# Router of a mixture-of-experts trunk: one chain over all tokens, and one chain per block of 128 tokens

## What is computed

```python
def hier_moe(h, w_rg, w_re, w_gate, w_up, w_down):
    t = h.reshape(b * s, d)
    pg = softmax(t @ w_rg);  pg_top, g_idx = top_k(pg, 1)          # the best of 4 groups
    le = (t @ w_re).reshape(-1, 4, 8)
    le_sel = take_along_axis(le, g_idx[:, :, None], axis=1)[:, 0]    # its 8 experts
    pe_top, e_idx = top_k(softmax(le_sel), 2)                        # the best two of them
    w = pg_top * pe_top / sum(pe_top)
    ids = g_idx * 8 + e_idx
    combine = sum(one_hot(ids, 32) * w[..., None], 1)
    a = silu(t @ w_gate[e]) * (t @ w_up[e]) * combine                # for all experts e
    return sum over e of a @ w_down[e]
```

## Time and profile before

| | us |
|---|---|
| median of 3 runs | 1030.28 (1030.17 to 1032.45) |
| the profiled execution | 1029.97 |
| its span, first to last instruction | 1028.3 |
| TensorE busy | 961.8 (94%) |
| VectorE busy | 575.5 (56%) |
| ScalarE busy | 428.9 (42%) |
| DMA moved | 313.02 MB, 304 GB/s on the mean |

### The profile page before, as it was taken

The page is one execution under the profiler, slowest core; times in us unless marked ns, Lnnn a source line. Parts: engine busy times, 40 slices in busy tenths (PEclk is TensorE's granted clock), DMA queues, the critical chain, the costliest instruction groups (busy, mean ns, idle before and its releaser), DMA issues.

```text
span 1028.3 us, 15490 instructions
## 1 busy us (share of the span) xinstructions
PE 961.8 (94%) x5906; PEld 670.8 (65%) x5906; DVE 575.5 (56%) x1184; ACT 428.9 (42%) x918; POOL 58.1 (6%) x74
## 2 busy tenths in 40 slices
PE   9999999999999995987999999999999999977877
PEld 7888877778886441533588887777788954344323
DVE  8656788896873231211276668898969533222212
ACT  5444566666443210210354355666664431111122
POOL 1120400000010000000004004000000100000000
PEclk9999999999999998998999999999999999989999
DMA  9975544247999999999998665342589999999996
GB/s 343 345 264 177 194 125 124 80 129 274 397 368 386 425 425 418 426 424 426 414 391 275 203 196 172 123 123 83 170 298 384 364 410 425 424 422 423 425 424 276
DMA packets 97114, 313.02 MB, mean 304 GB/s; under 512 B 13425, under 2 KB 18577, under 8 KB 74513
## 3 DMA queue, kind: packets, MB, share of 16 engines
q1 hardware_dynamic: 96704, 312.04, 80.0%
q10 hardware_dynamic: 336, 0.02, 0.0%
HBM read 310.20 MB, written 1.84 MB: 303 GB/s over the span
## 4 chain that ended last, share of the span: by engine, by line
PE 70%; DMA 10%; SPq 9%; DVE 6%; ACT 3%; issue 2%; POOL 0%; DVEq 0%; ACTq 0%; POOLq 0%
PE ps L1437 14%; PE ps L1439 14%; PE ps L1438 14%; SPq L484 9%; PE ps L2061 6%; DMA arena<-in_w_expert_up_dram 5%; DMA arena<-in_w_expert_gate_dram 3%; DMA ring_rest<-in_w_expert_down_dram 3%; PE ps L2147 2%; PE ps L2035 2%; PE ps L1462 2%; PE ps L2135 2%; ACT probs L966 2%; PE ps L1572 2%; PE ps L2006 1%
## 5 line engine op out<-in xcount | busy, mean ns | idle before, releaser
L1437 PE MATMUL ps<-whi,ahi 128*128 128x512 f32 (+1 forms) x736 | 284.4, 386 | 2.1 <-DVE arena L1109 1.1
L1090 DVE TENSOR_TENSOR wlo<-arena,whi 128x512 fp32r<-128x512 f32 (+1 forms) x352 | 233.0, 700 | 95.2 <-ACT whi L883 92.0
L1439 PE MATMUL ps<-whi,alo 128*128 128x512 f32 (+1 forms) x736 | 277.1, 377 | 0.0
L1438 PE MATMUL ps<-wlo,ahi 128*128 128x512 f32 (+1 forms) x736 | 276.8, 376 | 0.0
L883 ACT CAST whi<-arena 128x1024 fp32r<-128x1024 f32 (+1 forms) x171 | 175.5, 1028 | 176.6 <-PE ps L1439 168.0
L1437 PEld LDWEIGHTS ps<-whi,ahi 128*128 128x128 f32 x736 | 138.5, 188 | 31.1 <-issue 4.5
L1439 PEld LDWEIGHTS ps<-whi,alo 128*128 128x128 f32 x736 | 138.4, 188 | 25.6
L1438 PEld LDWEIGHTS ps<-wlo,ahi 128*128 128x128 f32 x736 | 138.7, 188 | 23.2
L2279 DVE SCALAR_TENSOR_TENSOR acts<-ps,wslot,acts 128x256 f32<-128x256 f32 x16 | 7.7, 484 | 169.9 <-ACT acts L1962 145.5
L2061 PE MATMUL ps<-arena,rows 128*32 128x512 f32 x416 | 90.7, 622 | 8.9 <-DMA arena<-in_w_expert_up_dram 7.3
L2061 PE MATMUL ps<-ring_rest,rows 128*32 128x512 f32 x352 | 76.6, 634 | 10.2 <-DMA arena<-in_w_expert_up_dram 10.2
(11 more groups left out here) (293 smaller groups left out, 1077.8 us busy)
## 6 DMA issues: line engine op xcount, KB each, us to landing
arena<-in_w_in_dram SPq DMA_DIRECT2D x62, 1024.0 KB, 5.4
arena<-in_w_expert_down_dram SPq DMA_DIRECT2D x38, 1024.0 KB, 20.5
arena<-in_w_expert_gate_dram SPq DMA_DIRECT2D x34, 1024.0 KB, 25.8
arena<-in_w_expert_up_dram SPq DMA_DIRECT2D x32, 1024.0 KB, 25.3
ring_rest<-in_w_expert_down_dram SPq DMA_DIRECT2D x24, 1024.0 KB, 18.9
ring_rest<-in_w_expert_gate_dram SPq DMA_DIRECT2D x22, 1024.0 KB, 25.8
ring_rest<-in_w_expert_up_dram SPq DMA_DIRECT2D x22, 1024.0 KB, 26.0
arena<-in_w_proj_a_dram SPq DMA_DIRECT2D x8, 1024.0 KB, 5.1
```

The lines of the kernel that those rows point to most:

```text
L1090: dve.tensor_tensor(wlo[:, jj % 2, cols], half_slot(jj, w)[:, cols], whi[:, jj % 2, cols].bitcast(F32), ALU.subtract).then_inc(low_split i ...
L1437: pe.matmul(o, hi, rhs_hi, start=first, stop=False)
L1438: pe.matmul(o, hi, rhs_lo, start=False, stop=False)
L1439: return pe.matmul(o, lo, rhs_hi, start=False, stop=last)
```

## The change

The routing works by token block.
- **Banks.** The logits of block tb lie in bank 4 + tb. Columns 6 and 7 are turned into banks of their own for each block (turned_last), evacuated per block by last_h2t_act and last_h2t_dve, and the router's products of columns 5, 6 and 7 are made first for block 0 and then for block 1. x_turned and logits_ready are raised per block. Two waits are new: part 2 of turn_new_x waits for h2t_ready 2, and the product of column 0 waits for h2t_odd 1 (column 2 did before).
- **Experts over all 32.** The expert logits of the other groups are lowered by 3e38 (others, lower), and MAX8 and the index search run over all 32. The picks are one-hots over 32, their sum is sel. gmask, the masked product, the reduction over the groups and either fall away.
- **Two chains.** Each step is made per block, and the steps of the two blocks alternate. link(ins, False) raises route_step without waiting, and each step waits for its own predecessor's count.
- **Ranks.** rank(tb) multiplies for each block, and TensorE makes block 0's rank after picked 1, adds block 0's totals in banks 4 and 7, and makes block 1's rank after picked 2.
- **Fillers.** WARM_ROUTE is 4 instead of 7; one filler is new between the two rankings.
- **Combine weights.** pick is multiplied in place over 32 and its two halves are added straight into comb.

```diff
-        idx_iota = sb("idx_iota", [P, PER_GROUP])
+        idx_iota = sb("idx_iota", [P, EXPERTS])
...
-            def link(ins):
+            def link(ins, hold=True):
                 count[0] += 1
                 ins.then_inc(s, 1)
-                eng.wait_ge(s, count[0])
+                if hold:
+                    eng.wait_ge(s, count[0])
+                return count[0]
...
-        WARM_SETUP, WARM_ROUTE, WARM_RANKS, WARM_LAST = 7, 7, 1, 1
+        WARM_SETUP, WARM_ROUTE, WARM_RANKS, WARM_LAST = 7, 4, 1, 1
...
+        def turned_last(k, tb):
+            return ps[:, ((7, 3), (6, 2))[k - (KB - 2)][tb], 0:P]
...
+        def last_h2t_act(act, l, tb):
+            act.wait_ge(x_turned, 4 + tb)
+            cols = slice(tb * P, (tb + 1) * P)
+            act.activation(h2t[:, KB - 2, cols], turned_last(KB - 2, tb), ACT.Copy,
+                           scale=second_gain(l, KB - 2)).then_inc(h2t_ready, 1)
+
+        def last_h2t_dve(dve, l, tb):
+            dve.wait_ge(x_turned, 4 + tb)
+            cols = slice(tb * P, (tb + 1) * P)
+            dve.tensor_scalar(h2t[:, KB - 1, cols], turned_last(KB - 1, tb), second_gain(l, KB - 1), None,
+                              ALU.mult).then_inc(h2t_odd, 1)
...
         def turn_new_x(pe, part, blocks=range(TB)):
+            if part == 2:
+                pe.wait_ge(h2t_ready, 2)
...
-        def router_part(pe, part, ks=None):
+        def router_part(pe, part, ks=None, blocks=range(TB)):
...
-                if k == 2 or k == KB - 1:
-                    pe.wait_ge(h2t_odd, 1 if k == 2 else 2)
-                elif k % 2 == 0:
-                    pe.wait_ge(h2t_ready, part + 1)
-                for tb in range(TB):
-                    mm = pe.matmul(ps[:, 4, tb * 64:tb * 64 + WR], h2t[:, k, tb * P:(tb + 1) * P], wr[:, k, 0:WR],
-                                   start=(k == 0 and tb == 0), stop=(k == KB - 1), skip_group_check=True)
+                for tb in blocks:
+                    if k == 0 or k == KB - 1:
+                        pe.wait_ge(h2t_odd, 2 + tb if k else 1)
+                    if k % 2 == 0 and k != 2:
+                        pe.wait_ge(h2t_ready, 3 + tb if part == 2 else part + 1)
+                    mm = pe.matmul(ps[:, 4 + tb, 0:WR], h2t[:, k, tb * P:(tb + 1) * P], wr[:, k, 0:WR],
+                                   start=(k == 0), stop=(k == KB - 1))
...
-                router_part(pe, 1, (5,))
-                router_part(pe, 2)
+                for tb in range(TB):
+                    router_part(pe, 1, (5,), (tb,))
+                    router_part(pe, 2, blocks=(tb,))
                 keep_clock(pe, WARM_ROUTE)
                 pe.wait_ge(picked, 1)
-                pe.matmul(ps[:, 6, 0:EXPERTS], before[:], sel[:, 0, :], start=True, stop=True)
-                pe.matmul(ps[:, 6, 64:64 + EXPERTS], before[:], sel[:, 1, :], start=True, stop=False)
-                pe.matmul(ps[:, 6, 64:64 + EXPERTS], ones[:], sel[:, 0, :], start=False,
-                          stop=True).then_inc(ranks_ready, 1)
-                pe.matmul(ps[:, 7, 0:EXPERTS], ones[:], sel[:, 0, :], start=True, stop=False)
+                pe.matmul(ps[:, 6, 0:EXPERTS], before[:], sel[:, 0, :], start=True, stop=True).then_inc(ranks_ready, 1)
+                pe.matmul(ps[:, 4, 0:EXPERTS], ones[:], sel[:, 0, :], start=True, stop=False)
+                pe.matmul(ps[:, 7, 0:EXPERTS], ones[:], sel[:, 0, :], start=True, stop=False)
+                keep_clock(pe, WARM_RANKS, 2)
+                pe.wait_ge(picked, 2)
+                pe.matmul(ps[:, 4, 0:EXPERTS], before[:], sel[:, 1, :], start=False,
+                          stop=True).then_inc(ranks_ready, 1)
...
+                def lower(tb, other):
+                    dve.wait_ge(route_step, other)
+                    return link(dve.scalar_tensor_tensor(
+                        out=grouped(lowered[:, tb, :]), in0=bcast(others[:, tb, :].unsqueeze(2), [P, GROUPS, PER_GROUP]),
+                        scalar=-3e38, in1=grouped(logits(tb, GROUPS, EXPERTS)), op0=ALU.mult, op1=ALU.add), False)
+
+                def best_experts(tb, low):
+                    dve.wait_ge(route_step, low)
+                    return link(dve.max(etop[:, tb, :], lowered[:, tb, :]), False)
...
+                step0 = copied(0)
+                step0 = best_group(0, step0)
+                step0 = group_index(0, step0)
+                step0 = other_groups(0, step0)
+                step0 = lower(0, step0)
+                step1 = copied(1)
+                step0 = best_experts(0, step0)
+                step1 = best_group(1, step1)
+                step0 = expert_index(0, step0)
+                step1 = group_index(1, step1)
+                step0 = picks(0, step0)
+                step1 = other_groups(1, step1)
+                selected(0, step0)
+                step1 = lower(1, step1)
                 dve.wait_ge(squares, 2)
-                link(dve.tensor_tensor(ss[:, 0, :], ss[:, 0, :], ss[:, 1, :], ALU.add))
-                link(dve.tensor_scalar(ss[:, 0, :], ss[:, 0, :], 1.0 / D, EPS, ALU.mult, ALU.add))
+                sums = link(dve.tensor_tensor(ss[:, 0, :], ss[:, 0, :], ss[:, 1, :], ALU.add), False)
+                step1 = best_experts(1, step1)
+                dve.wait_ge(route_step, sums)
+                means = link(dve.tensor_scalar(ss[:, 0, :], ss[:, 0, :], 1.0 / D, EPS, ALU.mult, ALU.add), False)
+                step1 = expert_index(1, step1)
+                dve.wait_ge(route_step, means)
                 dve.reciprocal(ss[:, 0, :], ss[:, 0, :]).then_inc(recips, 1)
+                step1 = picks(1, step1)
+                selected(1, step1)
...
+            def rank(dve, link, tb):
+                dve.wait_ge(ranks_ready, tb + 1)
+                link(dve.tensor_tensor(rk[:, tb, :], ps[:, 4 if tb else 6, 0:EXPERTS], sel[:, tb, :].bitcast(F32),
+                                       ALU.mult))
...
                     for tb in range(TB):
+                        if n == 0 and not routed:
+                            rank(dve, link, tb)
                         last = dve.tensor_tensor(onehot[:, n % 2, tb, :].rearrange("p (e c) -> p e c", e=4),
```

More of the change, by code:

```diff
@@ L155, in trunk_program @@
             top_i = sb("top_i", [P, TB, 8], U32, ctx)
-            gmask = sb("gmask", [P, TB, GROUPS], F32, ctx)
-            les = sb("les", [P, TB, 8], F32, ctx)
+            others = sb("others", [P, TB, GROUPS], F32, ctx)
             etop = sb("etop", [P, TB, 8], F32, ctx)
@@ L447, in rope_angles @@
             dve.tensor_copy(slot_iota[:], iota_i[:])
[L448 removed]
+            dve.tensor_copy(idx_iota[:], idx_iota_i[:])
         QUAD_LOADS = 12
@@ new lines, in route_dve, with logits, grouped, copied @@
+            def route_dve(dve, link):
+                def logits(tb, first, n):
+                    return ps[:, 4 + tb, first:first + n]
+                def grouped(t):
+                    return t.rearrange("p (g e) -> p g e", g=GROUPS)
+                def copied(tb):
+                    dve.wait_ge(logits_ready, tb + 1)
+                    return link(dve.tensor_copy(lg[:, tb, 0:GROUPS], logits(tb, 0, GROUPS)), False)
+                def best_group(tb, copy):
+                    dve.wait_ge(route_step, copy)
+                    return link(dve.max(top[:, tb, :], lg[:, tb, :]), False)
+                def group_index(tb, best):
+                    dve.wait_ge(route_step, best)
+                    return link(dve.max_index(top_i[:, tb, :], top[:, tb, :], lg[:, tb, :]), False)
+                def other_groups(tb, index):
+                    dve.wait_ge(route_step, index)
+                    return link(dve.tensor_tensor(others[:, tb, :], idx_iota[:, 0:GROUPS],
+                                                  bcast(top_i[:, tb, 0:1], [P, GROUPS]), ALU.not_equal), False)
+                def lower(tb, other):
[6 more added lines that the diff above has]
+                    return link(dve.max(etop[:, tb, :], lowered[:, tb, :]), False)
+                def expert_index(tb, best):
+                    dve.wait_ge(route_step, best)
+                    return link(dve.max_index(top_i[:, tb, :], etop[:, tb, :], lowered[:, tb, :]), False)
+                def picks(tb, index):
+                    dve.wait_ge(route_step, index)
+                    return link(dve.tensor_tensor(pick[:, tb, :, :], bcast(idx_iota[:].unsqueeze(1), [P, 2, EXPERTS]),
+                                                  bcast(top_i[:, tb, 0:2].unsqueeze(2), [P, 2, EXPERTS]),
+                                                  ALU.is_equal), False)
+                def selected(tb, pick_step):
+                    dve.wait_ge(route_step, pick_step)
+                    dve.tensor_tensor(sel[:, tb, :], pick[:, tb, 0, :], pick[:, tb, 1, :], ALU.add).then_inc(picked, 1)
+                link(dve.memset(lg[:], -3e38))
+                for tb in range(TB):
+                    last_h2t_dve(dve, l, tb)
+                step0 = copied(0)
```

(7 more changed lines are left out.)

68 lines of the change are left out of this document (14 added, 54 removed).

## The result

The changed kernel takes **1035.47 us** (median of 6 runs, 1034.58 to 1036.30) beside 1030.64 for the kernel before in the same measurement (6 runs, 1030.17 to 1032.45): ratio 1.0043, 95% interval 1.0033 to 1.0052. It is 4.8 us slower; 1.6 us faster had been forecast. Its profiled span is 1032.9 us, 4.6 above the 1028.3 of before.

What follows compares the result with a forecast made beforehand. The expert-weight stream was taken to end each stage. A gather 1.09 us earlier per layer was to close 0.85 and 0.75 us of its holes, 1.6 in all: 1028.7 us from a median of 1030.28, range 1027.5 to 1031.3.

Steps and rivals of the forecast that it cites:

- What bounds the kernel: Whole kernel: each expert stage ends when its weight stream ends; earlier routing can bring at most 1.88 us through the stream.
- Own banks and halves: Router's last part, split by block: block 0's logits ready at 313.8, VectorE starts at 313.84 instead of 314.80, 0.96 us earlier.
- The chains: VectorE routing steps of the two blocks alternate and overlap: picked 2 at 317.02 instead of 317.78, 0.76 us earlier.
- The chains don't overlap: Rival on VectorE's routing: each step stands alone, gather 0.6 us late, holes open by 0.6 a layer, 1031.5 us; chance 0.12.
- Ranks and gather: From picked 2 to first gather: block 0 ranked during chain 1, gather at 318.11, 1.09 us earlier per layer (0.65 to 1.25).
- From the gather to the end: Expert stages: SP's issues follow the earlier gather, close 0.85 and 0.75 us of lost streaming, in all 1.6 us.
- the holes: Slower stretches of the weight stream right behind the routing: 0.95 us of lost streaming in layer 0, 0.93 in layer 1.
- The wider iota and its copy lie in the setup: nothing: Setup: widening idx_iota and its copy was to cost nothing.
- Hidden anyway: Rival behind the routing: the holes stay whatever the issue's time, the stream ends where it did, 1030.3 us; chance 0.16.

Runs made afterwards that it cites:

- the old places: Changed kernel with idx_iota moved behind the last tile and 32 unused bytes where it stood, so weight tiles lie as in the kernel before: 1032.38 us.
- the moved ones: Changed kernel as it is (1035.47 us) against the kernel before with 96 unused bytes behind idx_iota (1034.40 us); tiles above idx_iota lie 96 bytes higher.

## Why the prediction was wrong

**What bounds the kernel: right.** The stream of expert weights ends each stage; all that changed the time in these runs changed the stream.

**Own banks and halves: right.** Block 0's copy was forecast at 313.84, with this trace's anchor (+0.76) 314.60; it starts at 314.56.

**The chains: nearly right.** They overlap with starts 0.10 to 0.12 apart; MAX8 and the index search over 32 experts take 0.20 and 0.18, over 8 in the same trace 0.15 to 0.17 and 0.16, against a forecast surcharge of 0.025. One row was not foreseen: the first `others` takes 0.40 us, the second only 0.15, in both layers. Picked 1 and 2 come at 316.87 and 317.98 where 315.92 and 317.02 plus the anchor's 0.76 make 316.68 and 317.78: 0.2 late, all of it in that row. "The chains don't overlap" is refuted. Of what the prediction quotes for it from the Trainium skill, "VectorE: DVE Perf Modes", section "The DRAIN you can't avoid", the exception, that a step that isn't held starts earlier, is what the trace shows for steps whose wait is already met.

**Ranks and gather: right.** From picked 2 to the gather 1.07 us, forecast 1.09. The gather is 0.91 earlier instead of 1.09, within the bounds 0.65 to 1.25. One reading was off without effect: 14 passes in 3.27 us are 0.23 each, not 0.217, and the eight that are left took 1.97 us, ahead of block 0's rank, which nobody waited for. TensorE's clock did not fall (granted clock 1.00 from 312.9 to 319.1 us), with 8 passes (315.03, 1.97 us) in place of the 14 of the earlier trace rows.

**"From the gather to the end": the step that failed.** SP's issue did follow: 10.94 us behind the anchor before, 10.03 after. The prediction then took the 2.0 us between an issue into an *idle* queue and full rate as the lead that any issue needs, and counted that the holes close by 0.85 + 0.75. The 2.0 us that it quotes beside this from the Trainium skill, "DMA: Bandwidth & Descriptors", section "Anatomy of one DMA — SWDGE (gpsimd) path", is another quantity: a fit to whole DMAs that GpSimd issues, most of it spent behind the last byte. That the two numbers agree supports nothing. With about 2.1 us queued ahead the load lands after 5.0 (before) and 5.3 us, with 3.0 ahead after 7.1 (after) and 7.4. At the old places the holes grew by 0.5 in each layer instead; in the changed kernel as it is, that of layer 0 did. The term of -1.6 us measured +1.9 at the old places and +1.1 at the moved ones. That the time of the issue is the cause is shown by holding SP's issues alone; why an earlier one fills the stream worse is open.

**"The wider iota and its copy lie in the setup: nothing": the second one.** The work is in the setup, but a tile is also an address. This edit, costed at nothing, is the largest term of the result, +3.1 us (+3.9 in the kernel before), and it slows a stream that isn't named in it. The range, 1027.5 to 1031.3, had no room for it.

**The rivals.** "Hidden anyway" had the right value for the gather's lead, zero, only where the issues are held, and the wrong reason: left alone, the holes get worse. None of the rivals had either cause of the slowdown.

## What to carry to other kernels

Before costing a change, compare where every tile that a saturated stream writes starts, before and after; here multiples of 256 bytes were worth up to 6.8 us of 1030 (1027.9 against 1034.7), more than the edit under study. An issue that comes earlier isn't always better: test the work and the issue apart by holding back the DMA alone. When a changed part is faster in the trace and the kernel slower, run the new code at the old places before explaining anything.

## What the runs showed of the hardware

- Rate of the stream from 330 to 390 us against where its tiles start in SBUF: 425 or 426 GB/s with at least one of the two tiles at a multiple of 256 bytes, 421 with neither, the same for offsets of 32, 96, 128 and 160 bytes. That the two tiles' costs don't add (0.5 to 0.8 and 3.2 to 4.2 us for the same ring_rest) has no explanation here.
- Time from issue to landing of the first 1024 KB load behind the routing in layer 0, against what was still queued: 4.7 us with 1.1 ahead; with 1.9 to 2.1 ahead 4.7 to 6.0 in twelve kernels and 6.4 and 6.5 in two; 6.7, 7.1 and 7.4 with about 3. The two groups nearly touch, so this is a tendency and no rule. Why a load waits longer when more is queued than its lead needs was not settled. The Trainium skill, "DMA: Bandwidth & Descriptors", section "Latency and other measured facts", puts most of the fixed cost down to the access time of HBM, which it gives as longer at high load; no run here separates that from the queue itself.
- The same load issued 1.1 us later behind an unchanged gather, in kernels whose stream sets the pace: 1032.38 became 1030.89 us, 1030.04 became 1028.19.
- VectorE's first `not_equal` compare of `idx_iota` with `top_i` in a layer takes 0.40 us in the changed kernel, the one behind it on the same kind of operands 0.15. The compare for equality of the same two tiles in the kernel before takes 0.17 (L1835, at 315.69). What makes the difference isn't known.
